# A two-layer hybrid diffusion step on one core: reordering the gated DeltaNet layer (opening, head loop, last head)

## What is computed

```python
def _gated_delta_chunked(q, k, v, g, beta, s0):      # per head, chunks of 64 tokens
    G = jnp.cumsum(g, axis=-1)
    decay = jnp.exp(jnp.where(causal, G[..., :, None] - G[..., None, :], -jnp.inf))
    kb = k * beta[..., None]
    lower = jnp.where(strict, jnp.einsum('nbhcd,nbhsd->nbhcs', kb, k) * decay, 0.0)
    sol = lax.linalg.triangular_solve(lower + eye, rhs=[v*beta, kb*exp(G)], ...)
    u, w = sol[..., :DV], sol[..., DV:]
    qk = jnp.where(causal, jnp.einsum('nbhcd,nbhsd->nbhcs', q, k) * decay, 0.0)
    def step(S, inp):
        v_new = uc - w @ S
        o = q_dec @ S + qk @ v_new
        S = g_end * S + k_end.T @ v_new
        return S, o

def _trunk(...):                                     # per layer
    mod = cs @ ada_w[layer] + ada_b[layer]           # six shifts, scales and gates
    hn = _rms_norm(x, norm1_g[layer]) * (1 + sc1) + sh1
    out, s = _gdn_mixer(hn, ...)   # q, k, v, z = projections; q, k, v: SiLU(3-tap convolution)
    x = x + g1 * out
    x = x + g2 * _moe(...)
```

## Time and profile before

| | us |
|---|---|
| median of three runs | 1501.41 |
| the three runs | 1501.41, 1495.56, 1515.63 |
| the profiled execution | 1497.87 |
| its span, first to last instruction | 1496.1 |

### The profile page before, as it was taken

One profiled execution on the slowest core, in us unless ns is written; L12 is line 12 of the kernel. 1 busy time (PEld: TensorE's weight loads), 2 busy tenths in 40 slices (PEclk: granted clock), 3 DMA queues, 4 the chain that ended last, 5 costly groups with the idle time before them and its releaser, 6 DMA issues.

```text
span 1496.1 us, 17316 instructions
## 1 busy us (share of the span) xinstructions
PE 1275.3 (85%) x6005; PEld 721.0 (48%) x6005; DVE 461.8 (31%) x1139; ACT 295.4 (20%) x622; POOL 323.5 (22%) x328
## 2 busy tenths in 40 slices
PE   3979999999996994989898758999999669987873
PEld 1447767766775654333333225666665523322321
DVE  0454555465543124000000044434332500100004
ACT  2234323332331121100000031111111200100001
POOL 0041223132211000333332102131320023332210
PEclk9979999999996895999998979999999679999997
DMA  9755535562554026698999862342410759999973
GB/s 383 302 203 210 214 89 182 199 207 72 217 195 152 4 103 283 259 355 300 419 390 428 358 248 97 108 145 89 146 49 16 288 233 391 355 429 427 427 329 136
DMA packets 91695, 352.99 MB, mean 236 GB/s; under 512 B 29136, under 2 KB 66832, under 8 KB 72592
## 3 DMA queue, kind: packets, MB, share of 16 engines
q0 software_dynamic: 20160, 188.77, 30.8%
q1 hardware_dynamic: 70144, 163.11, 29.9%
q10 hardware_dynamic: 1360, 0.71, 0.2%
HBM read 376.04 MB, written 21.60 MB: 266 GB/s over the span
## 4 chain that ended last, share of the span: by engine, by line
PE 68%; DMA 20%; DVE 5%; issue 2%; ACT 2%; SPq 1%; POOL 0%; POOLq 0%; DVEq 0%; ACTq 0%
DMA slot<-in_w_x,widx 14%; PE bank L1792 10%; PE bank L1267 10%; PE bank L663 8%; PE bank L1831 7%; PE bank L1187 6%; PE bank L744 3%; PE bank L345 3%; PE bank L671 2%; DMA slot<-in_ada_w 2%; PE bank L780 2%; PE bank L713 2%; PE bank L724 2%; PE bank L410 2%; PE bank L1591 1%
## 5 line engine op out<-in xcount | busy, mean ns | idle before, releaser
L1792 PE MATMUL bank<-slot,scr 128*64 128x512 f32 x1216 | 286.4, 629 | 37.0 <-DMA slot<-in_w_x,widx 35.3
L1792 PEld LDWEIGHTS bank<-slot,scr 128*64 128x64 f32 x1216 | 92.2, 145 | 228.3 <-issue 174.0
L1267 PE MATMUL bank<-hnT,slot 128*128 128x384 f32 x512 | 169.5, 488 | 3.5 <-DMA slot<-in_mlstm_w 2.1
L1831 PE MATMUL bank<-slot,scr 128*64 128x512 f32 x608 | 139.5, 612 | 26.4 <-DMA slot<-in_w_x,widx 19.0
L1267 PEld LDWEIGHTS bank<-hnT,slot 128*128 128x128 f32 x512 | 95.6, 190 | 67.4 <-DMA slot<-in_mlstm_w 2.3
L663 PE MATMUL bank<-hnT,slot 128*128 128x384 f32 x384 | 126.0, 488 | 0.0
L1934 POOL DMA_INDIRECT slot<-in_w_x,widx x102 | 102.3, 1003 | 60.7 <-POOL widx L1930 42.6
L1896 DVE TENSOR_TENSOR scr<-scr,bank 128x512 f32<-128x512 f32 x19 | 13.1, 687 | 307.0 <-PE bank L1792 307.0
L663 PEld LDWEIGHTS bank<-hnT,slot 128*128 128x128 f32 x384 | 72.3, 190 | 55.2 <-issue 6.5
L1831 PEld LDWEIGHTS bank<-slot,scr 128*64 128x64 f32 x608 | 46.9, 141 | 106.7 <-issue 91.0
L1187 PE MATMUL bank<-yT,slot 128*128 128x384 f32 x256 | 84.7, 493 | 0.7 <-DVE yT L1449 0.7
(11 more groups left out here) (283 smaller groups left out, 1681.2 us busy)
## 6 DMA issues: line engine op xcount, KB each, us to landing
slot<-in_ada_w SPq DMA_DIRECT2D x24, 2048.0 KB, 13.4
slot<-in_w_x SPq DMA_DIRECT2D x12, 2048.0 KB, 12.8
slot<-in_gdn_w SPq DMA_DIRECT2D x9, 2048.0 KB, 15.1
slot<-in_mlstm_w SPq DMA_DIRECT2D x16, 1024.0 KB, 6.9
scr<-rows_d SPq DMA_DIRECT2D x32, 384.0 KB, 4.3
slot<-in_w_out SPq DMA_DIRECT2D x2, 4096.0 KB, 15.4
slot<-inverse_d SPq DMA_DIRECT2D x16, 384.0 KB, 4.1
slot<-out_d SPq DMA_DIRECT2D x6, 1024.0 KB, 7.0
```

Source lines behind the costliest of these rows:

```text
L1267: mm = nc.tensor.matmul(bank[:, PROJ_BANK[s], 0:T], slot[:, 0, (s * KD + k) * P:(s * KD + k + 1) * P], hnT[:, k, :], start=(k == 0), stop= ...
L1792: mm = nc.tensor.matmul(bank[lanes[lane], m, :], xgT[:, k * P + lane * CAP:k * P + (lane + 1) * CAP], w_of[m][lane][:, k, :], start=(k == ...
L1831: mm = nc.tensor.matmul(bank[lanes[lane], 5 + h, :], hidT[:, k * P + lane * CAP:k * P + (lane + 1) * CAP], w_of[W_DOWN][lane][:, k, h * 51 ...
```

## The change

Edits in five places, all for layer 0:

1. *Opening, before the mixer.* The resets of the sums leave `const` for a small table on 16 partitions, loaded by ACT. PE waits for `const` alone and not for all small tables. The first norm is multiplied with `xT` first (`first_norm_dve`); scale and shift are put on afterwards, tiles 0, 2, 4, 6 by ACT and 1, 3, 5, 7 by DVE.
2. *Opening of the mixer.* The rows of the gates move to a place (`V`) that the convolution does not write. ACT convolves q and k of head 0 before it copies the columns. PE does columns and squares ahead of the second group of modulation products, and turns these behind `head(0)`; DVE copies and adds them later. SP loads head 1's weights ahead of two modulation blocks.
3. *Turn of the loop.* PE: `project(h + 1)` ahead of `modulation(h)`. ACT: `modulation(h)` behind `convolved(h + 1)`.
4. *Scan.* Six products of whole tiles write all values ahead of the first step, into banks shared by the two chains of a direction. The steps only add the state's term. The context chains now come first in `CHAINS`.
5. *Last head.* Parts 2 and 3 of the output projection are begun in `inverse(H - 1)`, between the turn of the modulation rows and the wait for the inverse; the last head's output goes to bank 4. The list on SP around `wout_sync` is as before.

The semaphores of the mLSTM are joined with those of the mixer, with their counts shifted.

```diff
@@ block_norm_act
+            if n == 0:
+                act.wait_ge(matrices_in, 16)
...
+            if n == 0:
+                act.wait_ge(dve_step, 2)
+                act.wait_ge(hn_scaled, KD)
+                for k in range(0, KD, 2):
+                    for g, lo, hi in SPANS:
+                        nc.scalar.activation(hnT[:, k, lo:hi], hnT[:, k, lo:hi], ACT.Identity,
+                                             scale=gain[:, 0, k, g:g + 1],
+                                             bias=mod[:, 0, 0, k, g:g + 1]).then_inc(hn_ready, 2)
...
+        def first_norm_dve(dve):
+
+            dve.wait_ge(rs_ready, 2)
+            for k in range(KD):
+                nc.vector.tensor_tensor(hnT[:, k, :], xT[:, k, :], rs[:, 0, :], ALU.mult).then_inc(hn_scaled, 1)
...
@@ gdn_pe
+                if isinstance(h, int):
+                    pe.wait_ge(g_y, 2 * H)
+                    wout_begin(pe, 0, EARLY_PARTS[:1])
+                    pe.wait_ge(g_mod, H)
+                    wout_begin(pe, 0, EARLY_PARTS[1:])
...
+                for g in range(N_DIR):
+                    for t in range(NT):
+                        us = slice((g * NT + t) * P, (g * NT + t + 1) * P)
+                        mm = nc.tensor.matmul(bank[:, *values_at(g, t)], DT[:, us], vb[:, us], start=(t < 2), stop=True,
+                                              skip_group_check=True)
+                        if t == 0:
+                            mm.then_inc(g_vps, 1)
+                    for ch, _, v, _ in now:
+                        _, d, cs = CHAINS[ch]
+                        c = cs[j]
+                        t, r = c // 2, (c % 2) * CHUNK
+                        S = state_of(ch, j)
+                        if S is None:
+                            continue
+                        if j > 0:
+                            pe.wait_ge(g_ssb, h * 10 + STATE_AT[(ch, j - 1)] + 1)
+                        nc.tensor.matmul(bank[r:r + CHUNK, *values_at(d, t)],
+                                         nwT[:, (d * NT + t) * P + r:(d * NT + t) * P + r + CHUNK], S, start=False,
+                                         stop=True, skip_group_check=True).then_inc(g_vps, 1)
...
             project(0, False)
+            pe.wait_ge(gate_dve, 3)
+            columns_pe(pe, (V[7], V[8], V[10], V[11]), 6)
+            squares(0)
             ada_products_pe(pe, 2)
             ada_products_pe(pe, 3)
-            pe.wait_ge(gate_dve, 3)
-            columns_pe(pe, (W[7], W[8], W[12], W[11]), 6)
-            squares(0)
-            ada_turn_pe(pe, 1)
             pe.wait_ge(cols_ready, 1)
             head(0)
+            ada_turn_pe(pe, 1)
             pe.wait_ge(mod_ready, 4)
             with pe.Fori(0, H - 1) as h:
+                project(h + 1, True)
                 modulation(h)
-                project(h + 1, True)
                 project_z(h)
                 squares(h + 1)
                 inverse(h)
-                scan(h)
+                scan(h, OUT_BANK)
@@ gdn_act
+            middle(0, 0)
+            middle(0, 1)
+            activated(0, 0)
+            activated(0, 1)
+            gdn_columns_act(act)
             act.wait_ge(cols_ready, 1)
             columns(0)
-            convolved(0)
+            middle(0, 2)
+            activated(0, 2)
+            nc.scalar.preload_act_table_set("natural_log_exp_and_others")
+            decays(0)
             squares_log(0)
             roots(0)
-            decays(0)
             with act.Fori(0, H - 1) as h:
                 state_decays(h)
-                modulation(h)
                 act.wait_ge(g_tok, h + 1)
                 columns(h + 1)
                 convolved(h + 1)
+                modulation(h)
                 output_gate(h)
                 squares_log(h + 1)
-                rest(h, True)
+                rest(h, True, OUT_BANK)
@@ gdn_dve
             convolved(0, Chain(dve, dve_step, base=begun))
-            ada_group_dve(dve, 1)
+            normalised(0, False)
+            ada_rows_dve(dve, 1)
             nc.vector.memset(blk, 0.0).then_inc(g_ors, 3)
-            normalised(0, False)
             head(0)
+            ada_mod_dve(dve, 1)
...
@@ gdn_sync
             rows(0)
             state(0)
+            sp.wait_ge(g_proj, 3)
+            weights(1)
             for i in range(2):
                 sp.wait_ge(ada_used, 7 + i)
                 modulations(2 * GROUP + i, i)
-            sp.wait_ge(g_proj, 3)
-            weights(1)
             sp.wait_ge(cleared_d, 32)
@@ the engines' lists
-                begun = ((1, 4), (0, 1, 2, 3))[layer]
+                begun = ((1, 5), (0, 1, 2, 3))[layer]
...
                     wout_begin(pe, layer, begun)
+                    begun += EARLY_PARTS
```

More of the change, by code:

```diff
@@ L65 @@
 C_RESET = C_BEFORE + P
-C_ROWDIR = C_RESET + 2 * N_DIR * T
+C_ROWDIR = C_RESET
 C_EPS = C_ROWDIR + N_DIR
@@ L129, in constants, with resets @@
     return c
+def resets():
+    t = np.arange(T)
+    rows = [t % length != edge for length in (CHUNK, P) for edge in (0, length - 1)]
+    return np.ascontiguousarray(np.tile(np.concatenate(rows).astype(np.float32), (N_DIR * H, 1)))
 def grid_positions():
@@ L621, in program @@
         cleared_d = sem("cleared_d")
-        g_ada_in = [sem(f"g_ada_in{i}") for i in range(2)]
         g_ada = sem("g_ada")
@@ L726, in inverse, with scan @@
                         mm.then_inc(g_ips, 1)
-            def scan(h):
+            def scan(h, out_bank):
                 for g in range(N_DIR):
@@ L743, in into_output @@
                 def into_output(lhsT, rhs, lo, hi):
-                    mm = nc.tensor.matmul(bank[:, 2, lo:hi], lhsT, rhs, start=first[0], stop=False,
+                    mm = nc.tensor.matmul(bank[:, out_bank, lo:hi], lhsT, rhs, start=first[0], stop=False,
                                           skip_group_check=True)
@@ L822, in gdn_pe @@
             inverse(H - 1)
-            scan(H - 1)
+            scan(H - 1, LAST_OUT_BANK)
             output_squares(H - 1)
@@ L870, in modulation, with rest @@
                 nc.scalar.activation(ada_rows[:, 0, :], bank[:, 3, :], ACT.Copy).then_inc(g_ada_sb, 1)
-            def rest(h, more):
+            def rest(h, more, out_bank):
                 for n in range(LEVELS - FIRST_LEVEL):
```

198 lines of the change are left out of this document (102 added, 96 removed).

## The result

The changed kernel took 1552.24 us (median of 4 runs, 1547.0 to 1556.8) against 1502.16 us for the kernel before on the same chip: a ratio of 1.035, 95% interval 1.031 to 1.039. Forecast were 1533 us with a range of 1515 to 1546, so the time lies 6 us above the range. The direction and the place of the loss were right, the size was not: the loss is 50 us instead of 36. The profiled run has a span of 1555.0 us, 58.9 us over the span of the earlier trace rows; it is the longest of the four (1556.8 us), so its trace shows some 9 us more than the medians do.

A forecast was written before the change was run, and what follows sets the result against it. The prediction took PE to bound the head loop, with next to no slack. Its terms, 36.9 + 8.4 - 8.8 - 2.9 + 2.0 = +35.6, on 1497.87 gave 1533 us, range 1515 to 1546.

The forecast's parts named there:

- What bounds the kernel: Head-loop turns: PE is busy 48.24 of 50 us, so whatever makes PE wait lengthens the turn one for one.
- Modulation behind the projections: Turns 1 to 6: z waits for ACT's copy behind the convolution, 6.15 us later a turn, +36.9 us in all.
- The clock behind the hole: Start of z in turns 1 to 6: lower clock after PE's wait, 1.4 us a turn, +8.4; bounds 0 and 11.4.
- rival E: Scan: values save little or the scan's clock falls; 1538 to 1545 us, chance 0.11.
- Values: Scan of each head: one product per tile saves 1.1 us a head, -8.8 us; bounds -2.4 and -12.8.
- Opening: Before the head loop's turns: smaller constants and reordered work start z of head 0 sooner, -2.9 us; bounds -1 and -5.
- the list behind the decays: Opening: durations summed from GpSimd's decays (3.8 us) through Exp, Ln, normalising, key products and DVE's head to head 1's projections at 91.3.
- Last head: Last inverse: early output projection waits for w_out until 487.2, then inverse at full clock; +2.0 us, bounds 0 and +11.
- Sum: Whole kernel: all terms together +35.6 us on the profiled run's 1497.87, giving 1533 us.
- D: Last head: clock stays low through the last inverse and scan; +9 us, 1542, chance 0.11.
- the 5.0 us of the page: Start of z in turns 1 to 6: low-clock cost by the skill page's estimate, 6 x 0.83 = 5.0 us, time 1529.

The follow-up runs named there:

- E1: Kernel before with only the loop's new order (PE: projections ahead of modulation; ACT: its copy behind the convolution): 1552.36 us, ratio 1.034.
- E2: Changed kernel with ACT's copy of the modulation rows moved up into the next head's convolution: 1508.54 us, ratio 1.005.
- E4: Changed kernel with eight unused z products (sixteen instructions) put in the hole ahead of z: 1542.17 us, ratio 1.026.
- E5: Kernel before with only the values change, one product per tile (six per head in place of twelve): 1496.21 us, ratio 0.998.
- E6: Kernel before with the new opening alone: 1501.55 us, ratio 1.002.
- E3: Changed kernel with the old loop order put back on PE and ACT; opening, values and last head stay: 1501.25 us, ratio 1.000.
- E7: E3 without the two early parts (28 instructions) of the output projection in the last head: 1499.32 us, ratio 0.999.
- E10: E3 with w_out loaded sooner and GpSimd's wait for the modulation products moved from ahead of its decays to its first write needing it: 1481.98 us, ratio 0.988.
- E12: E10 with four unused 128x384 products in each head's inverse; read by its turns only, 51.84 to 53.74 us.
- E11: E10 with the new order of the head loop kept: 1529.07 us, ratio 1.021.
- E8: E3 with w_out's load issued ahead of the last head's blocks: 1485.83 us, ratio 0.992.

## Why the prediction was wrong, step by step

- **What bounds the kernel.** Right: what made PE wait in a turn came out one for one (E1).
- **Modulation behind the projections: +36.9.** Right in mechanism and size. Third Silu, copy, z stood in that order in all turns; the hole was 5.31 us (5.5 said), and E1's turns are longer by 8.1 us, of which 6.15 remain when 2.0 are taken off for z. Shown by E1 (it alone is the loss) and E2 (the copy alone mends it).
- **The clock behind the hole: +8.4.** The mechanism was right, the size wrong, and the bound of 11.4 as well. z took 7.07 to 7.59 us in E1, and 7.3 to 8.4 in the changed kernel against 5.16: about 2.0 and 2.6 a turn in place of 1.4; E4 gives 2.1 to 2.4, or 13 to 15 us in all. The prediction took its price from 32 instructions of L345, behind a hole as long as the new one; the row with sixteen instructions like z's own, 7.03 for 5.16 in the earlier trace rows, stood beside it and gave 1.9 behind a hole half as long. The choice went by the hole, where the product was the better likeness. The estimate from the Trainium skill's page "TensorE: Matmul & The Clock Gate", section "HAM oscillation — how this bites in real kernels", was smaller still, 0.83 a turn; the runs do not agree with it in size, and the measurement, 2.4 to 3.1 times that, decides.
- **Clock elsewhere: 0 in the forecast.** Two of the turns of the changed kernel (60.1 and 60.3 us beside 57.5 to 57.8) and the one from z(6) on ran the end of their scan at low clock, about 2.4 us each, and turn 0 (60.2) a part of its inverse, 4.6 us more than before. The kernel before lost the end of its scan four times as well (three of the six turns, 1.7 to 1.9 us each, and the one from z(6) on), so most of the difference is the inverse. The chain of such a scan's end, and its stretch:

```profile
499.52 2.07 PE bank L805 x8
501.60 2.56 PE bank L730 x6
```

```profile
498.00:506.00 8.00, 7.35 (x30) 5.96 (x30) 1.72 (x4) 1.03 (x3) 0.77 (x1) 0.58 0.11 33
```

  The eight instructions of L805 take 1.14 us at full clock. The scan's end is rival E's mechanism, which had 0.11; an inverse in the loop was in no rival. What sets it off is open (below).
- **Values: -8.8.** Mis-sized. 0.7 to 0.8 us a head instead of 1.1 (from the last nwT product to the last output 11.79 us against 12.53), about 6 in all, of which the time kept 3 to 5 (E5, whose interval touches no change).
- **Opening: -2.9.** Wrong sign. The failed step is the list behind the decays: it leaves out ACT's table load (1.28), has 1.03 for a norm of 1.85, counts 1.4 for the low clock where the projections lost 2.8, and it starts from an opening 2.3 us sooner, of which 1.5 came. z(0) at 117.2 in place of 112.7. E6 puts the part at -1 to +6 us, its trace at +0.4.
- **Last head: +2.0.** Right in mechanism: PE waited 20.4 us in all for w_out, then ran the inverse and scan at full clock. The 28 early instructions took longer than said, 11.9 us for 10.6. E3 is 2 us above E7, as forecast, but inside the intervals.
- **Sum: the steps that failed.** 1552 is 19 us above 1533. Four of them are the base: the prediction added to a run of 1497.87, where the median is 1502.16. By the medians the change itself costs 50.1 us in place of 35.6, and the experiments divide the 14.5 that are missing. Some 5 are the order: 36.9 + 8.4 = 45.3 in the forecast, 50 in E1. The step that failed there is the clock behind the hole, 1.4 us a turn where 2.0 and more were measured. The other 9 to 10 are the -9.7 of values, opening and last head: E3 has just these three and gains nothing. The steps that failed there are the values, counted at 1.1 us a head where the trace shows 0.7, and the list of the opening, which forecast -2.9 where E6 shows no gain.
- **The same by the trace** of the longest run: the opening +4.6 against its forecast, turn 0 +5.1, turns 1 to 5 +5.5, z(6) to the projection's end +4.7, together 20 us over the 35.6. The clock has a part in all four. The range ended at 1546 since only the last inverse and scan were given a chance to lose the clock (D), and E was reckoned as an alternative to the forecast, where it came on top of it.
- **Slips in its sums.** 66.2 + 0.9 + 1.3 + 7.0 is 75.4 (75.3 said), 112.7 less 115.5 is -2.8 (-2.9), the time by the 5.0 us of the page is 1530 (1529), and the last head's inverse took 15.7 us up to the end of L733 (475.67 to 491.41), not 16.3. None of them matters for the miss.

**Open.** Why the clock falls in some inverses and scan ends and not in others. An inverse of the loop fell in seven of the thirteen kernels whose loop was read, one of seven each time and not always the same one, with PE busy throughout in the two shown (the changed kernel and E10); E12 does not tell what sets it off. The scan's end fell in none of the six turns of E1 and in four of E4. It may not be all chance: the changed kernel and E11 start z(0) 3.8 us apart, and in both the turns from z(2) and z(3) are the long ones (60.1 and 60.3 us, 60.0 and 60.3). No run separates its cause.

## What to carry to other kernels

Before moving a step later on one engine, find the bank or buffer that it frees and the first instruction elsewhere that waits for it, and count where in that engine's own order the freeing instruction now stands: with one 0.6 us copy put behind the convolution the kernel lost 50 us, and with the copy put back inside it 44 of them were there again. A hole on TensorE costs more than its length: price what is behind it by a row of the same products at low clock. And work put "into a wait" fills it only if its data are there: the 28 early instructions were worth nothing until their 4 MB load was issued 14 us sooner, and 10 (by the ratios) to 13 us (by the medians) then (E8 against E7).

## What the runs showed that was not expected

- Sixteen instructions of 5.16 us took 7.1 to 8.4 us behind an idle stretch of some 5.3 us; filling it with unused products brought them back to 5.2 to 5.4 (E4).
- An inverse of 64-column products (L767 and what follows) that starts at 0.50 stays there, though PE is busy for 15.5 of 16 us (E7). Behind 28 large instructions it starts and stays at 1.00 and takes 8.3 (E8).
- In turns whose inverse starts at full clock it can still fall in the middle of it with PE busy throughout: in the changed kernel's turn 0 the products L776 and L778 take 0.22 us a pair up to 127.2, and 0.43 from 127.5.

```profile
126.73 0.22 PE bank L778 x2
...
127.46 0.43 PE bank L776 x2
```
